# A two-layer pool/mLSTM block on one core: kept keys, per-bank releases and new orders in the mLSTM recurrence

## The reference, cut to what matters

```python
z = h @ w_in                                   # queries, keys, values, output gate o, 4 x 8 gates
h_f, _ = chunkwise(q, k, v, ig_f, lf_f, state_f)             # forward
h_b, _ = chunkwise(flip(q), flip(k), flip(v), ..., state_b)  # backward
y = (sigmoid(o) * (h_f + flip(h_b))) @ w_out

def chunkwise(q, k, v, ig, lf, state):         # for each head, chunk after chunk
    # within a chunk: s[t, s'] = (q[t] . k[s']) * exp(decay), num = s @ v, den = sum(s)
    # from the state: num += a[t] * q @ C,  den += a[t] * q . n
    h = num / max(|den|, exp(-m))
    # carried on: C = alpha * C + (k * w_end).T @ v,   n = alpha * n + sum(k * w_end)
```

## Time and profile before

| | |
|---|---|
| median of three runs | 2291.18 us (2291.17 to 2293.1) |
| profiled execution, its own time | 2294.48 us |
| its span, first to last instruction | 2292.6 us |
| PE busy, PE weight loads | 97%, 80% |
| DVE, ACT, POOL busy | 66%, 44%, 45% |
| mean granted TensorE clock | 0.986 |

### The profile page before, as it was taken

One profiled execution on the slowest core, in us unless ns is written; L12 is line 12 of the kernel. 1 busy time (PEld: TensorE's weight loads), 2 busy tenths in 40 slices (PEclk: granted clock), 3 DMA queues, 4 the chain that ended last, 5 costly groups with the idle time before them and its releaser, 6 DMA issues.

```text
span 2292.6 us, 35568 instructions
## 1 busy us (share of the span) xinstructions
PE 2214.4 (97%) x13230; PEld 1842.4 (80%) x13230; DVE 1502.1 (66%) x1999; ACT 1011.9 (44%) x1635; POOL 1023.5 (45%) x612
## 2 busy tenths in 40 slices
PE   7989999999999999999999999899999999999997
PEld 5657788888888889997899998777778888888885
DVE  5477566677798835464654626724677777888886
ACT  4654344444444455553433334333554444444443
POOL 0037677777600046661211025530498777771002
PEclk9999999999999999999999999989999999999998
DMA  8764442222382466534332247622212222228352
GB/s 341 250 230 165 156 138 82 83 83 82 103 320 74 165 234 232 178 129 151 126 113 71 98 142 221 218 74 74 74 53 84 81 82 81 110 98 292 128 175 101
DMA packets 123635, 326.32 MB, mean 142 GB/s; under 512 B 11376, under 2 KB 40816, under 8 KB 111216
## 3 DMA queue, kind: packets, MB, share of 16 engines
q1 hardware_dynamic: 105936, 299.35, 37.9%
q10 hardware_dynamic: 17568, 25.17, 3.0%
HBM read 269.82 MB, written 54.66 MB: 142 GB/s over the span
## 4 chain that ended last, share of the span: by engine, by line
PE 87%; DVE 3%; ACT 3%; DMA 3%; POOL 2%; issue 2%; ACTq 0%; SPq 0%; DVEq 0%; POOLq 0%
PE ps L1474 11%; PE ps L1476 11%; PE ps L1475 11%; PE ps L1104 6%; PE ps L1105 6%; PE ps L1603 6%; PE ps L1106 6%; PE ps L1605 6%; PE ps L1604 6%; PE ps L1647 2%; PE ps L1648 2%; PE ps L1649 2%; PE ps L1837 1%; PE ps L1242 1%; PE ps L1378 1%
## 5 line engine op out<-in xcount | busy, mean ns | idle before, releaser
L3174 DVE SCALAR_TENSOR_TENSOR acc<-ps,fcv,acc 128x945 f32<-128x945 f32 (+2 forms) x320 | 391.2, 1222 | 82.2 <-ACT acc L2354 49.6
L3931 POOL TENSOR_TENSOR w_lo<-raw,w_hi 128x2048 fp32r<-128x2048 f32 x36 | 170.1, 4726 | 381.9 <-ACT w_hi L2135 267.2
L3990 POOL TENSOR_TENSOR p_s_lo<-p_s_val,p_s_hi 128x512 fp32r<-128x512 f32 x160 | 243.0, 1528 | 116.2 <-ACT p_s_hi L2298 115.9
L1603 PE MATMUL ps<-da_hi,dw_hi 128*128 128x512 f32 x560 | 218.8, 391 | 0.0
L1604 PE MATMUL ps<-da_hi,dw_lo 128*128 128x512 f32 x560 | 218.1, 389 | 0.0
L1605 PE MATMUL ps<-da_lo,dw_hi 128*128 128x512 f32 x560 | 217.9, 389 | 0.0
L1647 PE MATMUL ps<-w_hi,hx_hi 128*128 128x256 f32 x512 | 145.9, 285 | 3.5 <-ACT stage L2707 3.4
L1648 PE MATMUL ps<-w_lo,hx_hi 128*128 128x256 f32 x512 | 144.8, 283 | 0.0
L1649 PE MATMUL ps<-w_hi,hx_lo 128*128 128x256 f32 x512 | 144.8, 283 | 0.0
L1603 PEld LDWEIGHTS ps<-da_hi,dw_hi 128*128 128x128 f32 x560 | 105.1, 188 | 23.0 <-issue 1.6
L1605 PEld LDWEIGHTS ps<-da_lo,dw_hi 128*128 128x128 f32 x560 | 105.1, 188 | 22.2
(11 more groups left out here) (521 smaller groups left out, 6505.3 us busy)
## 6 DMA issues: line engine op xcount, KB each, us to landing
f_raw<-in_ffn_w SPq DMA_DIRECT2D x25, 1024.0 KB, 5.0
modw<-in_modw SPq DMA_DIRECT2D x48, 512.0 KB, 8.0
raw<-in_ffn_w SPq DMA_DIRECT2D x23, 1024.0 KB, 5.0
a_scr<-fprod SPq DMA_DIRECT2D x40, 512.0 KB, 2.6
land_w<-in_ffn_w SPq DMA_DIRECT2D x40, 512.0 KB, 4.1
f_raw_b<-in_ffn_w SPq DMA_DIRECT2D x18, 1024.0 KB, 5.0
land_b<-a_scr SPq DMA_DIRECT2D x30, 512.0 KB, 5.0
raw<-in_mlstm_w SPq DMA_DIRECT2D x14, 1024.0 KB, 5.2
```

What stands on the lines that cost most here:

```text
L1603: pe.matmul(out, dw_hi[r][:, ws], da_hi[r][:], start=begins, stop=False, skip_group_check=True)
L3174: dve.scalar_tensor_tensor(out, src, cv[:, t:t + 1], out, ALU.mult, ALU.add).then_inc(sem("tap_done"), 1)
L3990: pool.tensor_tensor(p_lo[p][:], src, p_hi[p][:].bitcast(F32), ALU.subtract).then_inc(S.sem("lo_in"), 1)
```

## The change

1. **Kept keys.** The unweighted transposed keys of units 6 to 11 are copied by ACT from PSUM to SBUF (`keep_keys`). Units 12 to 17 visit the same chunks again; for them PE makes no transposes and DVE no `kw`: ACT multiplies the kept keys by the weights, 8 instructions of 64 columns (`weigh_kept_keys`), between the exponential and `g_hi` in its order.
2. **Banks freed one by one.** `hs_ready` is raised three times per unit; L1837's heads go bank by bank, each group behind its own count.
3. **Head order.** The state products run in the order 6, 1, 0, 3, 2, 5, 4, 7.
4. **Third rows.** `qa` buffer 2 moves out of the weights' region, so unit 6's rows are loaded before the last projection tile is done; unit 5's too go ahead of the values of unit 4.
5. **Last units.** Units 18 and 19 change places. `chunk_columns` is cut in three (behind units 17, 18 and the turn of 18), the output projection starts with 7 chunks turned, the last turn comes behind its first output tile, and the first projection weights are split by ACT behind unit 18 and by DVE ahead of the last `g_lo` and `back`.
6. **First loads.** Two `modm` halves are loaded before the projection, two of the next four a tile later; `masks` is loaded earlier.

```diff
-HALVES_LOADED = {3: (0, 6), 5: (6, 10), 7: (10, 14), ...}
+HALVES_LOADED = {3: (2, 4), 4: (4, 6), 5: (6, 10), 7: (10, 14), ...}
+STATE_ORDER = (6, 1, 0, 3, 2, 5, 4, 7)
-        qa = [... for i, o in enumerate((W_HI + 20480, W_HI + 22528, W_HI + 16384, W_HI + 18432))]
+        qa = [... for i, o in enumerate((W_HI + 20480, W_HI + 22528, EXT + 1024, W_HI + 18432))]
+        kept_keys = [at(f"kept_keys{c}", H_HI + 4096 * c, [P, 512]) for c in range(8)]
+        units[-2:] = [units[-1], units[-2]]
+        again = [u for u in second if u < carried]
+        by_bank = ((0, 2, 4), (1, 3, 5), (6, 7))
 # SyncE
+            for n in range(2):
+                chunk_half_in(n)
             sp.wait_ge(sem("pre_lo"), lows["x_pre1"] + 16)
...
             rows_in(x_units[0])
+            rows_in(x_units[1])
...
             values_in(4)
-            rows_in(x_units[1])
+            sp.wait_ge(sem("mod_sum"), 16 * (FT - 1))
+            rows_in(x_units[2])
             sp.wait_ge(sem("vo_done"), len(evacs))
             values_in(5)
-            rows_in(x_units[2])
 # TensorE
-                if u < carried:
+                if u < again[0]:
                     keys_turned(u)
...
-                    for h in range(HEADS):
-                        pe.matmul(num_of(h), dmat[:, i % 4, h, :], ...)
+                    for g, heads in enumerate(by_bank):
+                        if i >= 1:
+                            pe.wait_ge(sem("hs_ready"), 3 * (i - 1) + g + 1)
+                        for h in heads:
+                            pe.matmul(num_of(h), dmat[:, i % 4, h, :], ...)
                     if u >= 2:
                         turn(u - 2)
-                    for h in range(HEADS):
+                    for h in STATE_ORDER:
...
                 back(u)
+                if u == carried - 1:
+                    chunk_columns(0, 2)
+                if u == carried:
+                    chunk_columns(2, 8)
             turn(len(units) - 2)
-            chunk_columns()
-            turn(len(units) - 1)
-            pe.wait_ge(sem("glo_ready"), 8)
+            chunk_columns(8, HALVES // 2)
+            pe.wait_ge(sem("glo_ready"), 7)
...
+                    if h == 0 and d == 1:
+                        turn(len(units) - 1)
 # ScalarE
+            def weigh_kept_keys(u):
+                if u in again:
+                    act.wait_ge(sem("unit_done"), u - 1)
+                    for h in range(HEADS):
+                        act.activation(kw[u % 2][:, 64*h:64*h+64], kept_keys[n - 2][:, 64*h:64*h+64], ACT.Copy,
+                                       scale=cols[:, n, 1, c:c + 1])
...
                     decay(u + 1)
+                    keep_keys(u + 1)
+                    weigh_kept_keys(u + 1)
                 turned(u - 2)
+                if u == carried:
+                    hi_tile(K_MOUT)
 # VectorE
-                back(u)
-            turned(len(units) - 2)
+                if u < len(units) - 1:
+                    back(u)
+            dve.wait_ge(sem("num_done"), len(x_units))
             dve.wait_ge(sem("hi_in"), K_MOUT + 1)
             dve.tensor_tensor(w_lo[...], raw[...], w_hi[...], ALU.subtract).then_inc(sem("lo_in"), 1)
+            turned(len(units) - 2)
+            back(len(units) - 1)
```

More of the change, by code:

```diff
@@ L626, in build @@
         carried = len(units) - 2
+        again = [u for u in second if u < carried]
+        kept_units = [u for u in x_units if u not in second and units[u][1] in [units[v][1] for v in again]]
+        kept_index = {u: i for i, u in enumerate(kept_units)}
+        by_bank = ((0, 2, 4), (1, 3, 5), (6, 7))
+        assert kept_units == list(range(again[0] - len(again), again[0]))
         def keys_bank(u):
@@ L679, in in_use @@
                 got = [("vo_done", evac_of[t][-1] + 1)]
-                return got + ([("num_done", len(x_units)), ("hs_ready", len(x_units))] if t >= len(MSEQ) - 2 else [])
+                return got + ([("num_done", len(x_units) - (1 if t == len(MSEQ) - 2 else 0))] if t >= len(MSEQ) - 2 else [])
             return [("mo_part", 8 + 3 * (K - K_MOUT + 1))]
@@ L967, in _ @@
             sp.dma_start(al_scr, gend[0:64, 3, :]).then_inc(sem("rows_out"), 16)
+            sp.wait_ge(sem("cols_ready"), 4)
+            sp.dma_start(masks[:], a["masks"]).then_inc(sem("mask_in"), 16)
             sp.wait_ge(sem("rows_out"), ROWS_OUT)
@@ L1824, in back @@
                     pe.wait_ge(sem("qa_ready"), i + 1)
-                    if i >= 1:
-                        pe.wait_ge(sem("hs_ready"), i)
-                    pe.wait_ge(sem("state_ready"), 16 if i == 0 else 4 * (u - 1))
+                    pe.wait_ge(sem("state_ready"), 16 if i == 0 else 4 * carried if u == carried else 4 * (u - 1))
                     if i == 0:
@@ L1866, in turn, with chunk_columns @@
                 mm.then_inc(sem("turned"), 1)
-            def chunk_columns():
-                pe.wait_ge(sem("mod_sum"), 16 * (FT - 1))
-                pe.wait_ge(sem("state_zero"), SUMS_KEPT)
-                pe.wait_ge(sem("kw_ready"), carried)
-                for n, total in enumerate(msum[0:7] + msum_kept + msum[11:12]):
+            def chunk_columns(n0, n1):
+                if n0 == 0:
+                    pe.wait_ge(sem("mod_sum"), 16 * (FT - 1))
+                    pe.wait_ge(sem("state_zero"), SUMS_KEPT)
+                    pe.wait_ge(sem("kw_ready"), again[0])
+                    pe.wait_ge(sem("keys_kept"), KEPT_BASE + len(kept_units))
+                for n in range(n0, n1):
+                    total = (msum[0:7] + msum_kept + msum[11:12])[n]
                     for b in range(2):
@@ L3798, in back @@
                     if u in sec_index:
-                        for h in range(HEADS):
-                            src = num[:, h % 2, h // 2, 0:P] if h < 6 else num2[:, h - 6, 0:P]
-                            ins = dve.scalar_tensor_tensor(hs[:, n - 2, P * h:P * h + P], src, dens[:, 2, h:h + 1],
-                                                           hs[:, n - 2, P * h:P * h + P], ALU.mult, ALU.add)
-                        ins.then_inc(sem("hs_ready"), 1)
+                        for heads in by_bank:
+                            for h in heads:
+                                src = num[:, h % 2, h // 2, 0:P] if h < 6 else num2[:, h - 6, 0:P]
+                                ins = dve.scalar_tensor_tensor(hs[:, n - 2, P * h:P * h + P], src, dens[:, 2, h:h + 1],
+                                                               hs[:, n - 2, P * h:P * h + P], ALU.mult, ALU.add)
+                            ins.then_inc(sem("hs_ready"), 1)
                     else:
```

56 lines of the change are left out of this document (34 added, 22 removed), and 2 rows, old and new, of the table shared.

## The result

The changed kernel takes 2280.4 us (median of 5 runs, 2279.1 to 2282.74) where the kernel before takes 2293.1 us beside it (2291.17 to 2294.5): ratio 0.9946, 95% interval 0.9933 to 0.9958, so 12.4 us less, 9.6 to 15.4 by the interval. Forecast were 22.8 us less, 2268.4, with 2279 as the upper end of the range. The sign is right, the size is not.

The account below looks back on a forecast made before the run. PE, busy 97% of the span, was taken as the bound, so only time out of its row counts. Gains less charges summed to 22.8 us, from 2291.2 to 2268.4 us; range 2258 to 2279.

Parts of the forecast that it names:

- Last units, and the loop it starts from: Loop of units 14 to 17 falls to 7.58 us; unit 18 to 19 takes 7.2 instead of 9.66, 2.5 us gained.
- DMA: Units 12 and 13: full load queues take back 1.0 us, bounds 0 and 5.
- rival A: Loads pace the second visits, POOL waiting for `och` in most of them; about 2274 us, chance 13%.
- What stands behind the end: After the projection's start: new stall of about 4 us before the first square, 5.0 us lost; half clock 1.7 more.
- First loads: PE's gaps at 1042 and 1053 us shrink with loads moved ahead: 3.5 us gained, bounds 0 and 5.8.
- third rows: Units 4 and 5: unit 6's rows come earlier, so the whole excess of 5.4 us goes.
- head order: State products of units 4 to 11: all heads pair up, 0.6 us for each of 8 steps, 4.8 us gained.
- banks: Units 14 to 17: value products start bank by bank, loop 7.58 us instead of 8.31, 2.9 us gained.
- kept keys: From unit 12 on four transposes leave PE, which is the bound only up to unit 12: 0.6 us gained.
- the 6.2 us from unit 19 to the projection: From unit 19's state products to the output projection: 6.2 us instead of 16.0, 9.8 us gained.
- C: The end is free: ACT's work slips under the last turn, no half clock follows; 2259 us, chance 12%.
- D: PE gets half clock from unit 13 to the projection, slower than before; about 2303 us, chance 3%.

Follow-up runs that it names:

- all four edits: Changed kernel with unit 18's state wait moved behind the turn, end work reordered, output weights later, o chunks of units 12 and 13 earlier: 2266.17 us, 0.9887.

## Why the prediction was wrong

Most terms came out as worked out. The sum did not: it gave no time to a wait that the change had put in front of unit 18, and too little to the late o chunks and to what queues at the end.

- *Last units, and the loop it starts from.* The step that failed. I carried the loop's 7.58 us on to unit 18 and began the term of 7.2 us from there, with nothing for a wait. But with 18 and 19 exchanged, unit 18 = (1, 2) follows 17 = (1, 3) in the same direction and needs its state at once. The changed kernel has a wait for it (4 * `carried`), and it heads the value products: the rows in order showed `state_ready` first on L1857. DVE makes the state last, behind `dmat`. It cost 12.12 - 7.58 = 4.5 us in front of unit 18, and unit 19 took 9.93 - 7.2 = 2.7 us more, both partly at half clock. Moving the wait alone brought 17 to 18 down to 7.44 us and 18 to 19 to 8.34, 1.6 us less. The other 1.1 us are a half-clock stretch that begins there without a long gap as well; only the profile with all four edits lacks it (6.94), and what brings it stays open.
- *DMA.* Mis-sized: charged 1.0, measured 15.73 + 24.52 - 36.3 = 3.9 us in this profile. The mechanism was the one at the far bound (o chunks late), and rival A's sign, POOL waiting for `och`, came true in four of the eight units with a gate. What helped was the place in the queue: two chunks issued 3 and 2 units earlier made units 12 and 13 take 13.8 us (13.6 predicted), while 2 MB of weights issued later gave nothing in the whole and, in four profiles of seven, came with another chunk late. The fit by the Trainium skill that the prediction sets beside this term, page DMA: Bandwidth & Descriptors, section Anatomy of one DMA, is one for transfers issued by GpSimd, and the loads here are issued by SP; by it 512 KB would be an estimate of 3.2 us, and the o chunks' 512 KB took 7.5 in the median between 1415 and 1470 us.
- *What stands behind the end.* Charged 5.0, measured 6.2 (15.38 against 9.2). Missed was that the splits, with the square behind them, also wait for the low parts of the weights: POOL's stood behind the last gate until 1497.26, DVE's took until 1498.35, and this last one made the 1.05 us ahead of `p_g_hi`. The half clock of 6.83 us behind it cost 2.0 where 1.7 were charged. Nor was the stall a must: in another order it is 0.62 us.
- *First loads.* 3.5 forecast, 4.2 in the profile between the stage's first tile and unit 4, but undone they cost only 1.2 (not told from 0), and a half-clock stretch behind the gap at 1042, there in some executions and not in others, is worth 1.7 us. That gap stayed (1.95 us). Right in the sum, which is luck as far as these runs go: its cause is unproven.
- *Right as worked out:* third rows (5.4; undone 4.8), head order (0.54 to 0.6 for each of eight; 4.3 in the windows), banks (8.2 against 7.44 where 7.58 was worked out), kept keys (two steps of 0.59 where one was counted; ACT's eight small multiplications take 2.00 us, as chosen; the estimate by the Trainium skill, page ScalarE: Activation LUTs, section Rules for kernel authors, was 2.8, and the 0.4 us that the prediction puts beside it is what 2.8 exceeds the 2.35 in hand by in one unit, so 1.8 for four), and the 6.2 us from unit 19 to the projection (5.96).

In this profile the misses are 4.5 + 2.7 + 2.9 (DMA, beyond the 1.0) + 1.2 + 0.3, and 0.4 for what lies ahead of the stage, less 0.9 for the stretch to unit 4 (0.6), units 4 to 11 and the way from 19 to the projection, each a little better than forecast: 11.1, and 22.8 - 11.7 of span is 11.1. With the wait and the end's order put right the time is 2269.0, where 2268.4 was forecast for the change as it stood. That it lies so near is partly luck: units 12 and 13 still take 16.6 us there where 13.6 was forecast, and the way to the first square 10.8 where it was 14.2, two misses that cancel.

Of the rivals, C's free end was nearly there to be had by order alone (10.8 us against 9.2). D's sign, a window of units 13 to 18 under 0.9, did show (0.86), but not its mechanism: the half clock followed gaps and did not become lasting. The argument that 1.07 to 1.66 us gaps left the clock full holds for the kernel before alone: with the banks undone, gaps of 1.67 us were followed by half clock in two units of four. And it said nothing of the 3.4 us gap that the change made.

## What to carry to other kernels

When a change alters the order of units, write down for each unit which earlier result it needs and at which instruction the wait stands, above all at the seam where the pattern breaks; a wait belongs to the first instruction that uses what it waits for. Where an edit measures nothing in the whole, read the windows on both sides: the later weights gave 2.2 us in one and lost as much in its neighbours, and taking the known wait out first did not make the gain appear, since from its new place that load stood ahead of another one that was due sooner. Work queued on a helper engine ahead of what the busiest engine needs next is worth sorting by due time before the stall is booked as a cost.

## What was not expected of the hardware

- Idle time on PE costs more than its length. From 1370 us to the first square's product, in all fourteen profiles, each of the 15 gaps of 3.29 to 5.11 us on PE has a stretch of 3.41 or 6.83 us at 1.2 GHz beginning in it or within 0.7 us behind it; L1857 behind such a gap takes up to 3.8 us where it takes 2.05 at full clock. Shorter gaps went both ways: 2.24 us in front of unit 14 left the clock full in three profiles and not in a fourth. Undoing the banks cost 3 us by its gaps in units 14 to 17 and 3.3 more by the clock there.
- Loads differ between executions of the same code: 14 to 17, with the same instructions and loads, took 24.53, 24.20, 22.62 and 22.80 us in four profiles. The part ahead of the stage differs more: its first tile began between 1017.6 and 1023.4 us in fourteen profiles. Stages must be measured from a mark nearby, and terms under 2 us by medians.
- With the queues full SP itself stands: one issue of an o chunk took 5.25 us, at a DMA share of 1.09, where most take 0.65, and the weights behind it went out only at 1432.76. SP's queue in the changed kernel (start, time of the issue):

```profile
1427.46 5.25 SPq L1023 DMA_DIRECT2D och<-o_scr  x1
1432.76 0.43 SPq L725 DMA_DIRECT2D raw<-in_mlstm_w  x1
```
